# Stick-breaking turns and recurrence levels in one order, and a tail sum that is carried over the key blocks

## The reference, cut to what matters

```python
z = einsum('bhtd,bhsd->bhts', q, k) * scale
log_beta = log_sigmoid(z)
log_keep = where(valid, log_sigmoid(-z), 0.0)
log_tail = cumsum(log_keep, axis=3, reverse=True) - log_keep
w = where(valid, exp(log_beta + log_tail), 0.0)
out = einsum('bhts,bhsd->bhtd', w, v)
```

```python
decay = exp(where(causal, bc[t] - bc[s], -inf))
scores = einsum('bhtd,bhsd,bhtsd->bhts', q, k, decay)
o = scores @ v + (q * exp(bc)) @ state
state = exp(b_last) * state + (k * exp(b_last - bc)).T @ v
```

## Time and profile before

| | us |
|---|---|
| median of 3 runs | 1916.47 |
| lowest, highest | 1913.55, 1918.99 |
| the profiled execution: its time, its span | 1919.64, 1917.7 |
| TensorE busy | 1591.1 (83%) |
| VectorE busy | 764.8 (40%) |
| ScalarE busy | 334.2 (17%) |
| GpSimd busy | 263.4 (14%) |
| the stick-breaking stage, 1107.5 to 1232 | 124.5 |
| the recurrence stage, 1232 to 1324 | 92.0 |

### The profile page before, as it was taken

How to read it: one execution, slowest core, us unless ns; L and a number is a source line. 1 busy time by engine, 2 the same in 40 slices (tenths; PEclk the granted TensorE clock), 3 DMA queues, 4 the chain that set the end, 5 groups by cost and what they waited for, 6 DMA issues and landing times.

```text
span 1917.7 us, 18800 instructions
## 1 busy us (share of the span) xinstructions
PE 1591.1 (83%) x7524; PEld 1058.5 (55%) x7524; DVE 764.8 (40%) x1212; ACT 334.2 (17%) x555; POOL 263.4 (14%) x286
## 2 busy tenths in 40 slices
PE   5996999897999686977899988877878786888773
PEld 4785888775888332323688857766733232333331
DVE  6899635534364410114622267676420000101003
ACT  3310000115101110101311167432100000000001
POOL 0102003300000310101200014652020000000001
PEclk9998999999999797988899968988979998999997
DMA  4221232120246899998222100101789999999994
GB/s 174 76 99 66 66 103 96 66 88 1 66 153 250 263 401 427 427 427 338 91 83 80 58 1 1 45 1 46 310 276 429 429 431 428 429 431 429 430 418 163
DMA packets 54820, 412.05 MB, mean 215 GB/s; under 512 B 13888, under 2 KB 15168, under 8 KB 25936
## 3 DMA queue, kind: packets, MB, share of 16 engines
q1 hardware_dynamic: 45008, 394.05, 51.4%
q0 software_dynamic: 9728, 16.81, 2.4%
HBM read 402.40 MB, written 25.20 MB: 223 GB/s over the span
## 4 chain that ended last, share of the span: by engine, by line
PE 49%; DMA 26%; DVE 11%; ACT 4%; issue 4%; POOL 3%; SPq 2%; POOLq 0%; DVEq 0%; ACTq 0%
PE bank L1364 31%; PE bank L582 6%; DMA arena<-in_expert_in 5%; DMA ring<-in_expert_gate 5%; DMA ring<-in_expert_up 5%; PE bank L592 3%; DMA arena<-in_expert_gate 2%; DMA arena<-in_expert_up 2%; DMA arena<-in_expert_down 2%; DMA ring<-in_expert_down 2%; DMA arena<-in_expert_out 1%; DVE arena L2060 1%; DVE top L2059 1%; DVE ring_low L1955 1%; PE bank L1479 1%
## 5 line engine op out<-in xcount | busy, mean ns | idle before, releaser
L582 PE MATMUL bank<-arena 128*64 128x512 f32 x960 | 286.5, 653 | 84.9 <-DMA arena<-in_expert_up 22.2
L582 PEld LDWEIGHTS bank<-arena 128*64 128x64 f32 x960 | 97.3, 150 | 256.5 <-issue 254.0
L582 PE MATMUL bank<-ring,arena 128*64 128x512 f32 x576 | 183.9, 624 | 25.0 <-issue 8.7
L830 DVE TENSOR_TENSOR arena<-misc,bank 128x256 f32<-128x256 f32 (+1 forms) x32 | 17.7, 554 | 449.2 <-PE bank L582 306.7
L1954 DVE CAST ring_high<-ring 128x2048 fp32r<-128x2048 f32 x60 | 75.9, 1265 | 261.4 <-DMA ring<-in_stream_a 158.2
L1955 DVE TENSOR_TENSOR ring_low<-ring,ring_high 128x2048 fp32r<-128x2048 f32 x60 | 140.8, 2347 | 2.1
L592 PE MATMUL bank<-arena 128*64 128x512 f32 x448 | 114.4, 595 | 20.2 <-issue 12.8
L1364 PE MATMUL bank<-ring_low,xn_high 128*128 128x512 f32 x288 | 113.1, 393 | 0.0
L1364 PE MATMUL bank<-ring_high,xn_low 128*128 128x512 f32 x288 | 112.6, 391 | 0.0
L1364 PE MATMUL bank<-ring_high,xn_high 128*128 128x512 f32 x288 | 112.5, 391 | 0.0
L582 PEld LDWEIGHTS bank<-ring,arena 128*64 128x64 f32 x576 | 60.8, 144 | 88.9 <-issue 88.9
(11 more groups left out here) (372 smaller groups left out, 2954.2 us busy)
## 6 DMA issues: line engine op xcount, KB each, us to landing
ring<-in_stream_a SPq DMA_DIRECT2D x42, 1024.0 KB, 5.0
arena<-in_expert_gate SPq DMA_DIRECT2D x20, 2048.0 KB, 28.1
arena<-in_expert_up SPq DMA_DIRECT2D x20, 2048.0 KB, 28.7
arena<-in_expert_in SPq DMA_DIRECT2D x19, 2048.0 KB, 30.1
arena<-in_expert_down SPq DMA_DIRECT2D x18, 2048.0 KB, 28.8
ring<-in_expert_up SPq DMA_DIRECT2D x12, 2048.0 KB, 31.3
ring<-in_expert_down SPq DMA_DIRECT2D x12, 2048.0 KB, 28.2
ring<-in_expert_gate SPq DMA_DIRECT2D x12, 2048.0 KB, 30.3
```

Source lines behind the costliest of these rows:

```text
L582: last = nc.tensor.matmul(h[side * SLOTS:(side + 1) * SLOTS, :], tokens[:, k, side * SLOTS:(side + 1) * SLOTS], w[:, k * 512:(k + 1) * 512 ...
```

## The change

Two things are done at once.

One order: the recurrence has no loop of its own. Turn i (0 to 8) has four places, and after its own work each place of the turns 1 to 7 has the step n = 4(i-1) + place. Place 0: Z of head i (scores, absolute value, exp); place 1: R of head i-1 on TensorE, the log of head i on ScalarE, for i below 4 the running decay on VectorE; place 2: VectorE subtracts R of head i-1, makes the softplus of head i and its block sums, ScalarE takes exp of the weights of head i-1; place 3: SO of head i-1. `zw` has two buffers. The PSUM banks are split: Z, R and SO rotate over five, the recurrence over three. The last norm of the layer is now that of stick-breaking head 7. Buffers move (`diff`, `qE`, `kE`, `hsc` to the residual's place; `kd`, `kdR`, `qexp`, `states` to halves of the weight ring).

Carried sums: VectorE adds the softplus of block s+1 onto block s, from the last block to the first, in float32 (`sums_of_blocks`), so that R of block s needs two products: the triangle times block s, and the other triangle (`tri_lt`) times block s+1. That makes 9 float32 products for a head. The rounding (L1853) and the subtraction (L2460) are gone.

```diff
+STICK_BANKS, STATE_BANKS = (0, 1, 2, 3, 4), (5, 6, 7)
+PLACES = 4
+def step_after(i, place):
+    return PLACES * (i - 1) + place if 1 <= i < SBH else None
@@ TensorE
-            pe.wait_ge(sums_left_ready, 1)
-                    pe.wait_ge(sp_low_ready, g + 1)
-                        for s2 in range(s, NT2):
-                            for part_ in (sp_low, sp_high):
-                                last_ = nc.tensor.matmul(b[:, col:STICK_W[s]], left,
...
+            def sums_behind(g):
+                pe.wait_ge(sums_ready, g + 1)
+                for s in range(NT2):
+                    a, w = STICK_AT[s], STICK_W[s]
+                    b = begin2(("R", g, s))
+                    last_ = nc.tensor.matmul(b[:, 0:w], c("tri_ge"), sps[g % 2][:, a:a + w], start=True, stop=(s == NT2 - 1))
+                    if s + 1 < NT2:
+                        behind = STICK_W[s + 1]
+                        last_ = nc.tensor.matmul(b[:, w - behind:w], c("tri_lt"), sps[g % 2][:, a + w:a + w + behind],
+                                                 start=False, stop=True)
                     end2(last_)
...
+            for i in range(SBH + 1):
+                for place in range(PLACES):
+                    if place == 0 and i < SBH:
+                        scores(i)
+                    if place == 1 and i >= 1:
+                        sums_behind(i - 1)
+                    if place == 3 and i >= 1:
+                        stick_out(i - 1)
+                    if step_after(i, place) is not None:
+                        step(step_after(i, place))
+                    if i == SBH and place == 0:
+                        head_out(HGH - 1)
@@ ScalarE
-                    A.copy(sp_high[:, h % 2, :], sps[h % 2]).then_inc(sp_high_ready, 1)
+                    if place == 0 and i < SBH:
+                        stick_exp(i)
+                    if place == 1 and i < SBH:
+                        stick_log(i)
+                    if place == 2 and i >= 1:
+                        stick_weights(i - 1)
+                    if place == 3 and i >= 1:
+                        stick_copy(i - 1)
+                    if step_after(i, place) is not None:
+                        step(step_after(i, place))
@@ VectorE
+            def sums_of_blocks(v):
+                for s in range(NT2 - 2, -1, -1):
+                    a, w, behind = STICK_AT[s], STICK_W[s], STICK_W[s + 1]
+                    ins = V.tensor_tensor(v[:, a + w - behind:a + w], v[:, a + w - behind:a + w], v[:, a + w:a + w + behind],
+                                          ALU.add)
+                    if s > 0:
+                        then(ins)
+                ins.then_inc(sums_ready, 1)
...
+            for i in range(SBH + 1):
+                for place in range(PLACES):
+                    if place == 0 and i < SBH:
+                        stick_scores(i)
+                    if (i, place) == (0, 0):
+                        running_decay(0)
+                        keys()
+                    if place == 1 and 1 <= i < HGH:
+                        running_decay(i)
+                    if place == 2 and i >= 1:
+                        stick_subtract(i - 1)
+                    if place == 2 and i >= 2:
+                        head_sums(i - 2)
+                    if place == 2 and i < SBH:
+                        stick_logits(i)
+                    if step_after(i, place) is not None:
+                        step(step_after(i, place))
+                    if i == SBH and place == 0:
+                        level_read(STEPS - 1)
@@ GpSimd
-                    G.tensor_tensor(sp_low[:, h % 2, :], sps[h % 2], sp_high[:, h % 2, :].bitcast(F32), ALU.subtract)\
-                        .then_inc(sp_low_ready, 1)
+                if n + 2 < STEPS:
+                    level_diff(n + 2)
@@ SyncE
-                    sp.wait_ge(psum_filled2, U2.filled(("SO", SBH - 1)))
+                    sp.wait_ge(psum_filled2, U2.filled(("R", SBH - 1, NT2 - 1)))
```

More of the change, by code:

```diff
@@ L116, in read_before @@
     def read_before(self, key):
-        old = self.index[key] - BANKS
-        if old < 0:
+        i = self.index[key]
+        earlier = [n for n in range(i) if self.place[n] == self.place[i]]
+        if not earlier:
             return None, 0
+        old = earlier[-1]
         who = self.reader[old]
@@ L1620, in head_out, with step @@
                 end2(last_)
[L1622 to L1634, removed]
+            def step(n):
+                h, lv = divmod(n, LEVELS)
+                if lv == 0:
+                    pe.wait_ge(kd_ready, h + 1)
+                    transposes2(("KT", h), [kd[:, h % 2, t * P:(t + 1) * P] for t in range(NT)])
+                    b = begin2(("DG", h))
@@ new lines, in step @@
+                end2(last_)
+                if lv == 2:
+                    wait_read2(pe, ("KT", h))
+                    b = begin2(("KV", h))
+                    for t in range(NT):
+                        last_ = nc.tensor.matmul(b[:, t * P:(t + 1) * P], kdR[:, h % 2, t * P:(t + 1) * P],
+                                                 hv[:, t, h * HD:(h + 1) * HD], start=True, stop=True)
+                    end2(last_)
+                if lv == 1 and h >= 1:
+                    head_out(h - 1)
@@ new lines, in stick_subtract, with stick_logits @@
+            def stick_subtract(g):
+                for s in range(NT2):
+                    b = unit2(("R", g, s))
+                    zs = zw[g % 2][:, STICK_AT[s]:STICK_AT[s] + STICK_W[s]]
+                    read2(V.tensor_tensor(zs, zs, b[:, 0:STICK_W[s]], ALU.subtract))
+            def stick_logits(h):
+                dve.wait_ge(log_ready, h + 1)
+                then(V.scalar_tensor_tensor(sps[h % 2], zw[h % 2], 0.0, sps[h % 2], ALU.max, ALU.add))
+                sums_of_blocks(sps[h % 2])
@@ new lines, in step @@
+            def step(n):
+                h, lv = divmod(n, LEVELS)
+                if n + 2 < STEPS:
+                    level_diff(n + 2)
+                if h >= 1 and lv == 3:
+                    out_square(h - 1)
+                if h >= 1 and lv == 6:
+                    out_norm(h - 1)
+            for i in range(SBH + 1):
+                for place in range(PLACES):
+                    if place == 0 and i >= 2:
+                        head_square(i - 2)
+                    if place == 3 and i >= 2:
+                        head_norm(i - 2)
+                    if step_after(i, place) is not None:
+                        step(step_after(i, place))
+                    if (i, place) == (0, PLACES - 1):
+                        level_diff(0)
+                        level_diff(1)
+                    if i == SBH and place == 0:
+                        out_square(HGH - 1)
```

388 lines of the change are left out of this document (181 added, 207 removed).

## The result

| | median us | runs | ratio to the kernel before, 95% interval |
|---|---|---|---|
| before | 1917.73 | 4 | |
| after | 1950.13 | 4 (1947.17 to 1953.95) | 1.0172 (1.0153 to 1.0192) |

The change costs 32 us. The forecast was 1971 us, with a range of 1911 to 1996. The profiled execution of after took 1949.9 us, its span 1947.8. The windows of after show where it went. Columns as in the earlier trace rows; the first window is the whole of the changed stretch, from the first Z to the first mT. The granted clock is TensorE's, as a share of its full speed; half clock and full clock stand for stretches like 1195.69 to 1205.38 of after, where it was 0.50, and 1184.83 to 1189.80, where it was 1.00.

The account below looks back on a forecast made before the run. The bound was taken to be the handing over between in-order streams, no engine full. Start 15, turns 4 x 33 + 3 x 27.5, extras 20, end 21, -2 and +3 gave 271.5 against 216.5 us: +55, 1971 us, range 1911 to 1996.

Parts of the forecast that it names:

- 4 x 33 + 3 x 27.5: Seven turns: four of 33 us with Z at half clock, three of 27.5 with HO between, Z at full.
- I take it that the clock is at half from there until some 5 us after the next L and R began: TensorE, after its 5 us pause in each turn: half clock makes the turn 33 us, against 23 at full.
- R takes 7 us or more, not 5.5: Sign on TensorE: one head's R starts at half clock, 3 us at half and 4 at full.
- the 3 us of contention: VectorE's products meeting GpSimd's differences: some 3 us on the path, added to the sum.
- The pause of 5 us: TensorE idles between second and third level of each turn while VectorE does softplus and block sums; 4 to 6 us expected.
- the announced 27 to 34: Sign: from one scores block on VectorE to the next lie 27 to 34 us.
- the walk: Step-by-step timing of one turn of the new order: 23 us at full clock; wrong if turns are under 24 us.
- The moved loads: SyncE's last three halves of weights wait for the last R: no cost, under 5 us if it showed.
- (1): Rival: TensorE's clock stays as now, 0.81 on average; +24, 1940 us; chance 0.16.
- (2): Rival: the clock stays full despite the pauses; stages 214 us, no change, 1914 us; chance 0.08.
- (3): Rival: streams fill each other's gaps and VectorE bounds; 26 us less, 1890 us, turns below 23.5; chance 0.12.
- (4): Rival: the clock is never brought back in time, 33 us in all turns; +74, 1990 us; chance 0.08.

Follow-up runs that it names:

- the best order: Changed kernel with SO of the previous head ahead of the third level and Z of the next head ahead of the fourth on TensorE: 1896.16 us, ratio 0.9863.
- the order alone: Changed kernel with the old R: 30 fp32r products, rounding and subtraction kept, no block sums: 1930.66 us, ratio 1.0055.
- the carried sums alone: Kernel before, its two loops kept, with block sums on VectorE and 9 float32 R products, no rounding or subtraction: 1909.88 us, ratio 0.994.

## Why the forecast held in kind and was 21 us too high

Its sum was 15 + 235.5 + 21 = 271.5 us. The windows of after give 16.0 + 214.1 + 22.3 = 252.4. Beginning and end are within 1.3 us; the turns were forecast 21.4 us too long. The mis-sized term is 4 x 33 + 3 x 27.5, and the step behind it "I take it that the clock is at half from there until some 5 us after the next L and R began". By it SO was at half in all seven turns. In the four turns of 33 us Z was at half as well and R took 7.0; in the three of 27.5 Z was at full and R took 5.5.

- **The number of half-clock products.** SO was at half in four turns (6.08, 6.08, 6.07, 6.07 us) and at full in three (3.24, 3.27, 3.34); Z was at half in two (6.34) and at 3.28 in the others. By the forecast's own prices three SO at full are worth 3 x 2.5 us, and two turns fewer with Z at half 2 x 5.5, together 18.5 of the 21.4 us. The forecast let the clock come back behind HO alone, and no row of before showed that it does; it was my estimate. In after the clock was up again behind HO in turns 3 and 6 (0.50 over HO in turn 3 and 1.00 over the R products behind it; 0.50 and 0.97 over SO in turn 6), but also behind KV in turn 1 (0.50, then 1.00 over SO) and behind KT with DG in turns 2 (0.50, then 1.00 over Z) and 4 (0.50, then 0.99 over SO), as here:

```profile
1228.08 1.11 PE L1561 MATMUL bank<-cst,ring 128*128 128x128 f32 x4 [4.56 <-DVE ring L2402]
1228.99 1.91 PE L1672 MATMUL bank<-arena 128*128 128x128 f32 x8
1230.70 1.91 PE L1679 MATMUL bank<-resid 128*128 128x128 f32 x8
1232.40 3.27 PE L1649 MATMUL bank<-arena 128*128 128x64 f32 x28
```

- **R.** From its first start to the product behind it, it took 5.2 to 6.7 us, 41.4 in the seven turns. The forecast's sum holds 4 x 7.0 + 3 x 5.5 = 44.5 for it, and 3 us of the difference are already in the 2 x 5.5 above. It began at half in six turns and was at full after one or two products (in turn 2 they took 1.92 and 1.27 us and the third, as wide, 1.02). "R takes 7 us or more, not 5.5" was wrong.
- **How far this closes.** With the 3 us of contention below, 18.5 + 3 = 21.5 meets the 21.4, but as a sum only, and in part by luck. The forecast put KT with DG and KV on the path three times each, and the trace has four of each. Turn 5, where SO and Z were both at half and KV ran, took 31.5 us and not 33 + 1.8. What each turn saved was not measured apart.
- **The pause of 5 us** was there in every turn: 4.31, 4.30, 3.74, 4.56, 4.63, 4.68, 4.96. Block sums took 2.07 against 2.1 (the 0.05 for each linked wait in it stood in no row; the four adds lasted 0.69 to 0.77, 0.56, 0.43 and 0.29 in the mean), the absolute value 1.09 against 1.1. Turns were 27.9 to 32.4 us long, in the announced 27 to 34 (the last one counted to its HO), though one pause, 3.74, lies under the announced 4 to 6; the clock was 0.74, under the announced 0.75; VectorE was busy 60% of the stage, far from the 85% that would have refuted the walk.
- **GpSimd's differences** cost VectorE's products little: the first product of a level fell from 562 ns to 430, and one alone takes 420, so the 3 us set aside for it fall away. The forecast had compared the mean duration of 562 ns with a step of 0.34 us from start to start, where one alone lasts 0.41. The group over the whole stretch of after (busy us, mean ns, idle before):

```profile
L2358 DVE TENSOR_TENSOR resid<-resid,arena 128x256 f32<-128x256 f32 x28 | 12.0, 430 | 1.6 <-ACT resid L1919 1.0 <-DVE ring L2390 0.3 <-DVE resid L2381 0.2
```

- **The moved loads** cost nothing: 594.1 us behind the first mT, as before.
- **The rivals.** (1), an average clock of 0.81, gave 1940, 10 us under the result, and so was nearer than the forecast's 1971. Its mechanism isn't what is seen: the clock was 0.74, with half clock behind the long pauses. (2) asked what the order costs at a full clock, 214 us and 1914; filling the pauses gave 218.0 and 1917.8 at a clock of 0.93. So the walk was right within 4 us as a sum, though 7 of its 214 were contention that the 430 ns don't show, and most of what lies beyond it is the clock. (3) was placed in the pause between the second and the third level, to decide at a turn of 23.5 us. The place was right; what it takes is not faster sums but SO and Z moved into it. The mean turn was then 25.2 us with SO moved and 24.0 with both (1122.31 to 1273.31 and 1123.00 to 1267.20, six turns each). The kernel is faster than before already at 25.2, since the last turn and the end shrank as well: from the last scores block to the first mT 40.1 us (to 1313.4) against 50.2 in after (1303.49 to 1353.7). So 23.5 was set too low. (4), half in all turns, is refuted by three SO and four Z at full.

What the forecast didn't ask is what each part is worth without the other. It priced the removed rounding and subtraction at nothing in the new order's chain. That was right but for the three operations that last longer beside the subtraction there. It never said that half of the change would be a gain in the old order.

Open stays why a pause of 2.1 to 2.6 us is followed by the half clock in one turn and not in another: L took 1.16 us behind 2.59 in the best order and 2.08 behind 2.18 in after.

## What to carry to other kernels

When two independent chains are put into one order, write down for each wait of an in-order engine which ready work stands behind it: here moving SO and Z ahead of one wait each turned 1.7% slower into 1.2% faster with no work removed. Price the half clock behind each new pause of TensorE beside the pause (here SO at 6.08 instead of 3.24 us and Z at 6.34 instead of 3.28 behind 3.74 us), and test it with products that nobody reads: here these won 1.8%, and SO and Z in their place about 3%. A part that gains alone can cost in a new order, as the carried sums did (8.3 us of stage gained in the old order, 24.8 lost in the new), since what it removes may lie beside the path there while what it adds lies on it, so weigh the parts anew in each order.

## What the hardware showed beyond the forecast

- In turn 3 of after the granted clock stayed at half (0.50) from 1195.69 through L, SO, L and Z, 16.0 us of products without a gap, and through the first two products of R behind a further pause of 2.18. In four other turns it had risen behind L with KV (turn 1: 0.50 over KV, 1.00 over SO), KT with DG (turn 2: 0.50, then 1.00 over Z; turn 4: 0.50, then 0.99 over SO), or HO (turn 6: 0.50, then 0.97 over SO). It did not rise behind HO everywhere: at the end, from 1332.30, HO ran at 0.50 and so did the first product of R (1.91 us), and the third took 1.02. Why it rose behind some products and went on at half over SO and Z is not shown.
- The clock also fell in the middle of SO. In the last turn of the order with SO and Z early the granted clock was 1.00 when SO began, behind a wait of 1.32 us, and stayed there to 1282.20; it was 0.50 from 1282.80 to 1284.40, and the level behind it took 2.02. Why it fell there is open.

```profile
1280.23 4.19 PE L1649 MATMUL bank<-arena 128*128 128x64 f32 x28 [1.32 <-ACT arena L1911]
```

- Pauses shorter than I had reckoned with matter: in turn 3 of after, behind 2.47 us at a granted clock of 1.00, the level took 1.32 at 0.90 and HO 0.63 a pair at 0.50, the half clock, and filling these pauses alone won 0.7%.
- In the order alone VectorE's product of two operands in SBUF took 4.18 us beside GpSimd's subtraction of 3.96, against 0.42. In before an absolute value took 4.56 us beside a subtraction of 4.00 (L2460, from 1162.56). In the carried sums alone, which have no subtraction, all eight absolute values took 1.09. Why they lasted longer there is not shown; the change took these cases away.
